# Chunk scores of the HGRN2 layer: one 32-column key stationary per chunk, in its own strip of output partitions, with the decays on the queries

## The chip, the cores and the metric

The kernel runs on one core of one Trainium2 chip. The metric is the time of one execution on the device, in microseconds (us); before the change it is 1723.18 us, the median of three runs.

## The reference, cut to what matters

A trunk of two layers over 512 tokens and a model width of 1024, in float32. Layer 0 (called layer 1 in the words of the change) is an HGRN2 gated linear recurrence with 16 heads of 128, in chunks of 32 tokens; layer 1 is a dilated attention, which the change does not touch. For one head and one chunk the recurrence is

```python
def step(state, xs):
    q_c, k_c, lf_c, v_c = xs
    b = jnp.cumsum(lf_c, axis=2)          # log of the forget gate, summed inside the chunk
    b_last = b[:, :, -1:, :]
    q_dec = q_c * jnp.exp(b)
    scores = jnp.einsum('bhcd,bhsd->bhcs', q_dec, k_c * jnp.exp(-b))
    scores = jnp.where(causal, scores, 0.0)
    o = (jnp.einsum('bhcs,bhse->bhce', scores, v_c)
         + jnp.einsum('bhcd,bhde->bhce', q_dec, state))
    state = (jnp.exp(b_last[:, :, 0, :])[..., None] * state
             + jnp.einsum('bhcd,bhce->bhde', k_c * jnp.exp(b_last - b), v_c))
    return state, o
```

The kernel works on blocks of 128 tokens, four chunks each. Inside a block it computes the scores of each chunk's queries against the keys of its own and of all earlier chunks, so the decays of the whole chunks in between have to be put on one of the two operands. The state is carried from block to block.

## The kernel before, in words

**Layout.** S = 512 tokens are ST = 4 blocks of P = 128; a block has NC = 4 chunks of CH = 32. Channels lie on the partitions, tokens run along the free axis. The 16 heads go in four rounds ("quads") of HQ = 4; `quads` (L258) loops over three rounds and writes the last one out separately (`last`).

**TensorE.** Nearly all of its work is `split_matmuls` (L418, its matmul is L422): every projection is three matmuls, with weights and activations each split into a high and a low part of type fp32r, 512 columns at a time. A head has three projection tiles, forget gate (F), query (Q) and gate (G), each computed in two halves of 12 matmuls (`head_tile`). Between the halves, `hg_body` (L610) calls `recurrence` (L599) for the head before: `scores` (L558) after the first half of F, `updates` (L572) after the second, `outputs` (L580) after the first half of Q, `norm_sum` (L593) after the second. For the last head of a round the same four stand between halves of value or output projections. `scores` has 16 matmuls of full f32: for block b and chunk j the stationary is `keys[:, b, j, 0:seen]` with seen = 32, 64, 96 or 128 key columns, the moving operand is the 32 queries of chunk j. Then three transposes (L569) turn `keys[:, b, 4, :]`, the keys decayed to the block's end, for the state update.

**VectorE and ScalarE.** Per head, ScalarE computes the forget gate, its log and its exponentials `eb` and `enb` (lines L837 to L852), VectorE the running sum (`cumulate`, L1153) and then `decays` (L1156), which makes the queries `qd`, `qs` and the four versions of the keys that `scores` reads: `keys[:, b, j, :]` holds the keys decayed up to chunk j. `A`, the decay of one whole chunk, is the last column of `eb` of that chunk. Then `mask_scores` (L1122) copies the scores out of PSUM with the causal mask, and `states` (L1132) carries the state. Each engine works through its own list in the order in which it is written, `decays` is followed by `split_lo` (L1017, the low part of a weight tile) and, further on, by `gate` and `mask_scores`. `link` makes VectorE wait for its own last result through a semaphore; there are 11 of them per head.

**What waits for what.** `scores` waits for `keys_ready` (the last of the key products, L1177), `kT_copy` on ScalarE (L802) for the transposes, `updates` for that copy, `outputs` for `q_ready`, `sT_ready` and `state_ready`. The two exponentials of a head are followed by `decays`, whose start also comes behind `hg_output` of the head before, which waits for `norm_sum` through ScalarE (L815, L817).

Of the kernel before, what the change touches and what calls it, by code (L numbers as in the profile page):

```python
# [31 lines left out]
ALU = mybir.AluOpType  # L32
# [4 lines left out]
P = 128  # L37
S = 512
# [3 lines left out]
H = W // P  # L42
HQ = 4
NQ = H // HQ
ST = S // P
# [72 lines left out]
LINKS_HG = 4 * 11  # L118
# [7 lines left out]
def program(nc, x, ln_g, hg_w_in, hg_lb, hg_norm, hg_w_out, at_w_in, at_w_out, rel_bias, final_g,  # L126
            consts, onehot, relmask, out):
    ctx = ExitStack()
    with ctx:
# [42 lines left out]
        ef, fg, kk, lnf, bb, eb, enb, qd, qs, sT = [rows[:, i, :] for i in range(10)]  # L172
        keys = sb("keys", [P, ST, NC + 1, P])
        dec = sb("dec", [P, ST, NC + 1])
# [24 lines left out]
        relmask_sb = keys[:, :, :, :].rearrange("p a b c -> p (a b c)")[0:H, 0:GROUPS * EXT]  # L199
        ext_sb = keys[:, :, :, :].rearrange("p a b c -> p (a b c)")[0:H, GROUPS * EXT:2 * GROUPS * EXT]  # L200
# [38 lines left out]
        q_ready, keys_ready, scores_done, sT_ready = sems("q_ready keys_ready scores_done sT_ready")  # L239
        kT_done, kT_ready, U_done, state_ready = sems("kT_done kT_ready U_done state_ready")  # L240
# [176 lines left out]
        def _(pe):  # L417
# [140 lines left out]
            def scores(g):  # L558

                pe.wait_ge(keys_ready, g + 1)  # L560
                for b in range(ST):
                    for j in range(NC):

                        seen = (j + 1) * CH
                        ins = nc.tensor.matmul(p_sc[0:seen, b * P + j * CH:b * P + (j + 1) * CH], keys[:, b, j, 0:seen],  # L565
                                               qd[:, b * P + j * CH:b * P + (j + 1) * CH], start=True, stop=True)
                ins.then_inc(scores_done, 1)
                for b in range(ST - 1):
                    ins = nc.tensor.transpose(p_kT[:, b * P:(b + 1) * P], keys[:, b, NC, :], ident[:, :])  # L569
                ins.then_inc(kT_done, 1)  # L570
# [9 lines left out]
            def outputs(g, h):  # L580

                pe.wait_ge(q_ready, g + 1)
                pe.wait_ge(sT_ready, g + 1)
                pe.wait_ge(state_ready, g + 1)
                for b in range(ST):
                    s = slice(b * P, (b + 1) * P)
                    ins = nc.tensor.matmul(p_O[:, s], v_sb[0][:, b, h * P:(h + 1) * P], sT[:, s],  # L587
                                           start=True, stop=(b == 0))
                    if b:
                        ins = nc.tensor.matmul(p_O[:, s], state[:, b - 1, :], qs[:, s], start=False, stop=True)  # L590
                ins.then_inc(O_done, 1)
# [424 lines left out]
        def _(dve):  # L1016
# [84 lines left out]
            step(nc.vector.memset(dec[:, :, :], 1.0))  # L1101
# [30 lines left out]
            def states(link, g):  # L1132

                dve.wait_ge(U_done, g + 1)
                link(nc.vector.tensor_copy(state[:, 0, :], p_U[:, 0:P]))
                link(nc.vector.scalar_tensor_tensor(out=state[:, 1, :], in0=state[:, 0, :], scalar=dec[:, 1, NC:NC + 1],
                                                    in1=p_U[:, P:2 * P], op0=ALU.mult, op1=ALU.add))
                nc.vector.scalar_tensor_tensor(out=state[:, 2, :], in0=state[:, 1, :], scalar=dec[:, 2, NC:NC + 1],
                                               in1=p_U[:, 2 * P:3 * P], op0=ALU.mult, op1=ALU.add)\
                    .then_inc(state_ready, 1)  # L1140
# [15 lines left out]
            def decays(link, q, h, g, low_before):  # L1156
# [5 lines left out]
                nc.vector.tensor_tensor(qd[:, :], proj[bank][:, :], eb[:, :], ALU.mult).then_inc(bank_free[bank], 1)  # L1162

                flat = keys[:, :, :, :].rearrange("p b s k -> p b (s k)")
                own = bass.AP(flat.tensor, flat.offset, [list(flat.ap[0]), [(NC + 1) * P, ST], [P + CH, NC], [1, CH]])
                after = bass.AP(flat.tensor, flat.offset + P, [list(flat.ap[0]), [(NC + 1) * P, ST], [P + CH, NC], [1, CH]])
                link(nc.vector.tensor_tensor(own, chunk(kk), chunk(enb), ALU.mult))
# [3 lines left out]
                link(nc.vector.tensor_tensor(after, own, A.broadcast_to([P, ST, NC, CH]), ALU.mult))  # L1171

                link(nc.vector.tensor_copy(dec[:, :, 1:2], A[:, :, 0, :]))

                for j in range(1, NC):
                    link(nc.vector.tensor_tensor(dec[:, :, j + 1:j + 2], dec[:, :, j:j + 1], A[:, :, j, :], ALU.mult))
                    ins = nc.vector.tensor_tensor(keys[:, :, j + 1, 0:j * CH], keys[:, :, j, 0:j * CH],  # L1177
                                                  A[:, :, j, :].broadcast_to([P, ST, j * CH]), ALU.mult)
                    if j < NC - 1:
                        link(ins)  # L1180
                    else:
                        ins.then_inc(keys_ready, 1)
                nc.vector.tensor_tensor(chunk(qs), chunk(qd), dec[:, :, 0:NC].unsqueeze(3).broadcast_to([P, ST, NC, CH]),
                                        ALU.mult).then_inc(q_ready, 1)
# [271 lines left out]
```

## Time and profile before

| | |
|---|---|
| three runs | 1716.9, 1723.18, 1723.3 us; median 1723.18 |
| span of the profiled execution, first to last instruction | 1719.9 us; its time as a run is not given apart from the three above |
| TensorE matmul busy | 1696.3 us, 99% |
| TensorE weight load busy | 1446.8 us, 84% |
| VectorE busy | 798.4 us, 46% |
| ScalarE busy | 642.7 us, 37% |
| mean granted TensorE clock | 0.982 of full speed |
| HBM traffic | 89 GB/s over the span |

The recurrence lies in the first 580 us. The busy time of TensorE is a modelled one, since matmuls overlap, so the argument below reads starts and the chain of waits, not busy shares. In the chain a matmul of full f32 is two passes of the array, two instructions; a projection matmul is one.

### The profile page before, as it was taken

The numbers are of one execution on the slowest core, as the hardware profiler recorded it, in microseconds if no ns is written. First come the engines' busy times: TensorE is split into PE (matmuls) and PEld (weight loads), VectorE is DVE, ScalarE is ACT, GpSimd is POOL, SyncE is SP. The second block draws the span as 40 slices with busy tenths as digits, with TensorE's granted clock in tenths as the row PEclk, the third lists the DMA queues.
The fourth block names the chain that finished last, engine by engine and source line by source line (L and its number), as shares of the span: only waits on it lengthen the run. The fifth ranks groups of instructions, "written<-read, shape, count | busy, mean of one in ns | idle before, by whom it ended". The sixth has DMA issues, their size and how long they took to land.

```text
span 1719.9 us, 22142 instructions
## 1 busy us (share of the span) xinstructions
PE 1696.3 (99%) x8249; PEld 1446.8 (84%) x8249; DVE 798.4 (46%) x1363; ACT 642.7 (37%) x1088; POOL 20.8 (1%) x40
## 2 busy tenths in 40 slices
PE   7999999999999999999999999999999999999997
PEld 6888888888888689888899888889888889888886
DVE  6564574556465632444433344442344442334445
ACT  4443354343344333343332333333233333233333
POOL 0000000000000000000000000000000000000000
PEclk9999999998998999999999999999999999999999
DMA  6522321321321124433314323332333333333321
GB/s 208 158 69 73 92 64 45 110 73 61 91 69 61 39 85 117 98 81 84 89 54 122 98 62 87 91 86 91 113 93 80 93 68 98 98 93 82 87 54 62
DMA packets 247998, 149.47 MB, mean 87 GB/s; under 512 B 47040, under 2 KB 227648, under 8 KB 247920
## 3 DMA queue, kind: packets, MB, share of 16 engines
q1 hardware_dynamic: 203328, 139.69, 29.4%
q0 software_dynamic: 2608, 8.39, 1.5%
q10 hardware_dynamic: 41984, 0.27, 1.3%
q8 instruction: 59, 0.97, 0.2%
q14 instruction: 19, 0.16, 0.0%
HBM read 146.02 MB, written 6.50 MB: 89 GB/s over the span
## 4 chain that ended last, share of the span: by engine, by line
PE 97%; DVE 1%; ACT 1%; issue 0%; DMA 0%; SPq 0%; DVEq 0%; ACTq 0%
PE proj L422 80%; PE inner L565 4%; PE inner L686 3%; PE inner L654 2%; PE inner L422 2%; PE inner L674 2%; PE inner L642 1%; PE inner L587 1%; PE inner L590 1%; PE inner L576 1%; PE inner L569 0%; DMA v<-x 0%; DVE v L1405 0%; PE inner L544 0%; PE inner L531 0%
## 5 line engine op out<-in xcount | busy, mean ns | idle before, releaser
L1023 DVE TENSOR_TENSOR w_lo<-raw,w_hi 128x1024 fp32r<-128x1024 f32 x252 | 308.0, 1223 | 483.2 <-ACT w_hi L735 482.1
L422 PE MATMUL proj<-u_hi,w_hi 128*128 128x512 f32 x1280 | 514.6, 402 | 0.0
L422 PE MATMUL proj<-u_hi,w_lo 128*128 128x512 f32 x1280 | 503.1, 393 | 0.0
L422 PE MATMUL proj<-u_lo,w_hi 128*128 128x512 f32 x1280 | 503.0, 393 | 0.0
L735 ACT ACTIVATE w_hi<-raw 128x1024 fp32r<-128x1024 f32 x252 | 265.3, 1053 | 133.6 <-PE proj L422 118.5
L422 PEld LDWEIGHTS proj<-u_hi,w_lo 128*128 128x128 f32 x1280 | 243.1, 190 | 52.7
L422 PEld LDWEIGHTS proj<-u_lo,w_hi 128*128 128x128 f32 x1280 | 243.7, 190 | 48.7
L422 PEld LDWEIGHTS proj<-u_hi,w_hi 128*128 128x128 f32 x1280 | 243.4, 190 | 48.8 <-issue 0.3
L422 PE MATMUL proj<-w_hi,u_hi 128*128 128x512 f32 x472 | 191.8, 406 | 6.7 <-issue 3.7
L422 PE MATMUL proj<-w_lo,u_hi 128*128 128x512 f32 x472 | 189.2, 401 | 0.0
L422 PE MATMUL proj<-w_hi,u_lo 128*128 128x512 f32 x472 | 188.9, 400 | 0.0
L422 PEld LDWEIGHTS proj<-w_hi,u_hi 128*128 128x128 f32 x472 | 121.8, 258 | 18.9 <-issue 8.9
L422 PEld LDWEIGHTS proj<-w_hi,u_lo 128*128 128x128 f32 x472 | 121.8, 258 | 9.4
L422 PEld LDWEIGHTS proj<-w_lo,u_hi 128*128 128x128 f32 x472 | 122.1, 259 | 8.5
L969 ACT ACTIVATE qk<-proj 128x512 f32<-128x512 f32 x96 | 57.0, 594 | 161.7 <-PE proj L422 161.7
L899 ACT ACTIVATE rows<-rows,negm 128x256 f32<-128x256 f32 (+1 forms) x128 | 61.9, 484 | 140.8 <-DVE negm L1303 135.6
L422 PE MATMUL proj<-y_hi,w_hi 128*128 128x512 f32 x256 | 103.4, 404 | 0.9 <-DVE sg L1112 0.7
L422 PE MATMUL proj<-y_lo,w_hi 128*128 128x512 f32 x256 | 100.2, 391 | 0.0
L422 PE MATMUL proj<-y_hi,w_lo 128*128 128x512 f32 x256 | 100.1, 391 | 0.0
L741 ACT ACTIVATE v<-proj 128x512 f32<-128x512 f32 x59 | 35.1, 596 | 138.8 <-PE proj L422 127.2
L1205 DVE TENSOR_TENSOR hT<-hT,proj 128x512 f32<-128x512 f32 x80 | 54.4, 686 | 69.0 <-PE proj L422 68.7
L565 PEld LDWEIGHTS inner<-rows,keys 128*32 128x32 f32 (+3 forms) x512 | 53.6, 156 | 13.1 <-issue 5.3
(156 smaller groups left out, 1497.0 us busy)
## 6 DMA issues: line engine op xcount, KB each, us to landing
raw<-at_w_in SPq DMA_DIRECT2D x160, 512.0 KB, 4.1
raw<-hg_w_in SPq DMA_DIRECT2D x64, 512.0 KB, 4.2
raw<-hg_w_out SPq DMA_DIRECT2D x16, 512.0 KB, 3.6
raw<-at_w_out SPq DMA_DIRECT2D x16, 512.0 KB, 4.4
v<-x SPq DMA_DIRECT2D x4, 512.0 KB, 6.5
bias_tiles<-ext_rows POOLq DMA_DIRECT2D x1, 2048.0 KB, 11.8
bias_tiles<-ext_rows POOLq DMA_DIRECT2D x2, 1024.0 KB, 17.6
bias_n<-bias_tiles POOLq DMA_DIRECT2D x16, 128.0 KB, 4.1
```

Source lines behind the costliest of these rows:

```text
L422: ins = nc.tensor.matmul(bank[:, :], stationary(a), moving(b), start=(first and n == 0), stop=(last and n == 2))
L565: ins = nc.tensor.matmul(p_sc[0:seen, b * P + j * CH:b * P + (j + 1) * CH], keys[:, b, j, 0:seen], qd[:, b * P + j * CH:b * P + (j + 1) * ...
L576: ins = nc.tensor.matmul(p_U[:, b * P:(b + 1) * P], kT[:, b, :], v_sb[0][:, b, h * P:(h + 1) * P], start=True, stop=True)
L654: ins = nc.tensor.matmul(p_S[r // 2][:, ((r % 2) * 2 + i) * P:((r % 2) * 2 + i + 1) * P], qk[:, 2 + 2 * i, s], qk[:, 3 + 2 * i, s], start= ...
L674: ins = nc.tensor.transpose(p_T[n % 2][:, (i % 4) * P:(i % 4 + 1) * P], src, ident[:, :])
L686: ins = nc.tensor.matmul(o, vals, pT[:, i, :], start=(i == 0), stop=(i == len(TILES) - 1), skip_group_check=True)
L735: nc.scalar.activation(w["hi"][:, slot, :], raw[:, slot, :], ACT.Copy).then_inc(hi_ready, 1)
L741: nc.scalar.activation(v_sb[group][:, (e - (0 if q is None else layer.heads)) % ST, :], value_bank(layer, q, e)[:, :], ACT.Copy).then_inc( ...
L899: nc.scalar.activation(probs[:, i, 0:n], probs[:, i, 0:n], ACT.Exp, bias=negm[:, i:i + 1], accum_out=stat[:, i // ST, 1, b:b + 1]).then_in ...
L969: nc.scalar.activation(o, src, ACT.Copy, scale=QSCALE if i in (Q0, Q1, Q2) else 1.0)\
L1023: nc.vector.tensor_tensor(w["lo"][:, slot, :], raw[:, slot, :], w["hi"][:, slot, :].bitcast(F32), ALU.subtract).then_inc(w_ready, 1)
L1205: nc.vector.tensor_tensor(hT[:, k, :], hT[:, k, :], proj[bank][:, :], ALU.add)\
```

## The change

Each chunk's keys are made once, decayed to the end of their own chunk (`aft`), and stand in TensorE once per block: 32 columns, whose results go to the 32 output partitions of that chunk. They meet the queries of their own chunk and of all later ones in one matmul, 128, 96, 64 or 32 columns. The decays between chunks are on the queries: `qx[:, b, r, j, :]` is chunk j's queries with the decays of the r − 1 chunks before it (r = 0: with the own chunk's decay divided out again, by `undo`), and the moving operand takes r = 0 for the own chunk, 1, 2, 3 for later ones: n pieces of 32 with a step of 160 elements (`q_steps`). The keys at the block's end, `kend`, are made apart and have a semaphore of their own (`kend_ready`), for which TensorE waits between the scores and the transposes. `outputs` reads `q_steps(b, 1, 0, NC)` in place of `qs`. Nothing else in the order of the work changes.

```diff
 Q0, K0, Q1, K1, Q2, K2, GA = range(7)
-LINKS_HG = 4 * 11
+LINKS_HG = 4 * 5
 LINKS_AT = 4 * 7
...
         rows = sb("rows", [P, 10, S])
-        ef, fg, kk, lnf, bb, eb, enb, qd, qs, sT = [rows[:, i, :] for i in range(10)]
-        keys = sb("keys", [P, ST, NC + 1, P])
-        dec = sb("dec", [P, ST, NC + 1])
+        ef, fg, kk, lnf, bb, eb, enb, kend, spare_row, sT = [rows[:, i, :] for i in range(10)]
+
+        qx = sb("qx", [P, ST, NC + 1, NC, CH])
+        aft = sb("aft", [P, S])
+        tail = sb("tail", [P, ST, NC + 1])
+        undo = sb("undo", [P, ST, NC])
...
+        def q_steps(b, r, j, n):
+
+            at = ((b * (NC + 1) + r) * NC + j) * CH
+            return bass.AP(qx_flat.tensor, qx_flat.offset + at, [list(qx_flat.ap[0]), [(NC + 1) * CH, n], [1, CH]])
...
+        kend_ready = sem("kend_ready")
...
                 pe.wait_ge(keys_ready, g + 1)
                 for b in range(ST):
-                    for j in range(NC):
-
-                        seen = (j + 1) * CH
-                        ins = nc.tensor.matmul(p_sc[0:seen, b * P + j * CH:b * P + (j + 1) * CH], keys[:, b, j, 0:seen],
-                                               qd[:, b * P + j * CH:b * P + (j + 1) * CH], start=True, stop=True)
+                    for c in range(NC):
+
+                        own = slice(c * CH, (c + 1) * CH)
+                        to = p_sc[own, b * P + c * CH:(b + 1) * P].rearrange("p (j c) -> p j c", c=CH)
+                        ins = nc.tensor.matmul(to, aft[:, b * P + c * CH:b * P + (c + 1) * CH],
+                                               q_steps(b, 0, c, NC - c), start=True, stop=True)
                 ins.then_inc(scores_done, 1)
+                pe.wait_ge(kend_ready, g + 1)
                 for b in range(ST - 1):
-                    ins = nc.tensor.transpose(p_kT[:, b * P:(b + 1) * P], keys[:, b, NC, :], ident[:, :])
+                    ins = nc.tensor.transpose(p_kT[:, b * P:(b + 1) * P], kend[:, b * P:(b + 1) * P], ident[:, :])
                 ins.then_inc(kT_done, 1)
...
                     if b:
-                        ins = nc.tensor.matmul(p_O[:, s], state[:, b - 1, :], qs[:, s], start=False, stop=True)
+                        ins = nc.tensor.matmul(p_O[:, s].rearrange("p (j c) -> p j c", c=CH), state[:, b - 1, :],
+                                               q_steps(b, 1, 0, NC), start=False, stop=True)
                 ins.then_inc(O_done, 1)
...
+            step(nc.vector.memset(tail[:, :, :], 1.0))
...
                 link(nc.vector.tensor_copy(state[:, 0, :], p_U[:, 0:P]))
-                link(nc.vector.scalar_tensor_tensor(out=state[:, 1, :], in0=state[:, 0, :], scalar=dec[:, 1, NC:NC + 1],
+                link(nc.vector.scalar_tensor_tensor(out=state[:, 1, :], in0=state[:, 0, :], scalar=tail[:, 1, 0:1],
                                                     in1=p_U[:, P:2 * P], op0=ALU.mult, op1=ALU.add))
-                nc.vector.scalar_tensor_tensor(out=state[:, 2, :], in0=state[:, 1, :], scalar=dec[:, 2, NC:NC + 1],
+                nc.vector.scalar_tensor_tensor(out=state[:, 2, :], in0=state[:, 1, :], scalar=tail[:, 2, 0:1],
                                                in1=p_U[:, 2 * P:3 * P], op0=ALU.mult, op1=ALU.add)\
                     .then_inc(state_ready, 1)
...
                 A = chunk(eb)[:, :, :, CH - 1:CH]
                 dve.wait_ge(proj_done, number + 1)
                 dve.wait_ge(eb_ready, 2 * g + 2)
-                nc.vector.tensor_tensor(qd[:, :], proj[bank][:, :], eb[:, :], ALU.mult).then_inc(bank_free[bank], 1)
-
-                flat = keys[:, :, :, :].rearrange("p b s k -> p b (s k)")
-                own = bass.AP(flat.tensor, flat.offset, [list(flat.ap[0]), [(NC + 1) * P, ST], [P + CH, NC], [1, CH]])
-                after = bass.AP(flat.tensor, flat.offset + P, [list(flat.ap[0]), [(NC + 1) * P, ST], [P + CH, NC], [1, CH]])
-                link(nc.vector.tensor_tensor(own, chunk(kk), chunk(enb), ALU.mult))
+                grown = undo[:, :, :].unsqueeze(3).broadcast_to([P, ST, NC, CH])
+                qstep = lambda r: qx[:, :, r, r - 1:NC, :]
+                nc.vector.tensor_tensor(qstep(1), chunk(proj[bank]), chunk(eb), ALU.mult).then_inc(bank_free[bank], 1)
+                nc.vector.reciprocal(undo[:, :, :], A[:, :, :, 0])
+                nc.vector.tensor_copy(tail[:, :, 3:4], A[:, :, 3, :])
+                link(nc.vector.tensor_tensor(aft[:, :], kk[:, :], enb[:, :], ALU.mult))
                 if low_before:
                     y_low(g - 1, h - 1)
 
-                link(nc.vector.tensor_tensor(after, own, A.broadcast_to([P, ST, NC, CH]), ALU.mult))
-
-                link(nc.vector.tensor_copy(dec[:, :, 1:2], A[:, :, 0, :]))
-
-                for j in range(1, NC):
-                    link(nc.vector.tensor_tensor(dec[:, :, j + 1:j + 2], dec[:, :, j:j + 1], A[:, :, j, :], ALU.mult))
-                    ins = nc.vector.tensor_tensor(keys[:, :, j + 1, 0:j * CH], keys[:, :, j, 0:j * CH],
-                                                  A[:, :, j, :].broadcast_to([P, ST, j * CH]), ALU.mult)
-                    if j < NC - 1:
-                        link(ins)
-                    else:
-                        ins.then_inc(keys_ready, 1)
-                nc.vector.tensor_tensor(chunk(qs), chunk(qd), dec[:, :, 0:NC].unsqueeze(3).broadcast_to([P, ST, NC, CH]),
-                                        ALU.mult).then_inc(q_ready, 1)
+                nc.vector.tensor_tensor(qx[:, :, 0, :, :], qstep(1), grown, ALU.mult)
+                nc.vector.tensor_tensor(tail[:, :, 2:3], tail[:, :, 3:4], A[:, :, 2, :], ALU.mult)
+                nc.vector.tensor_tensor(chunk(aft), chunk(aft), A.broadcast_to([P, ST, NC, CH]), ALU.mult)
+                link(nc.vector.tensor_tensor(qstep(2), qx[:, :, 1, 1:NC, :],
+                                             A[:, :, 0:NC - 1, :].broadcast_to([P, ST, NC - 1, CH]), ALU.mult))
+                nc.vector.tensor_tensor(tail[:, :, 1:2], tail[:, :, 2:3], A[:, :, 1, :], ALU.mult)
+                nc.vector.tensor_tensor(qstep(3), qx[:, :, 2, 2:NC, :],
+                                        A[:, :, 0:NC - 2, :].broadcast_to([P, ST, NC - 2, CH]), ALU.mult)\
+                    .then_inc(keys_ready, 1)
+                dve.wait_ge(keys_ready, g + 1)
+                nc.vector.tensor_tensor(tail[:, :, 0:1], tail[:, :, 1:2], A[:, :, 0, :], ALU.mult)
+                nc.vector.tensor_tensor(chunk(kend), chunk(aft),
+                                        tail[:, :, 1:NC + 1].unsqueeze(3).broadcast_to([P, ST, NC, CH]), ALU.mult)\
+                    .then_inc(kend_ready, 1)
+                nc.vector.tensor_tensor(qstep(4), qx[:, :, 3, 3:NC, :],
+                                        A[:, :, 0:NC - 3, :].broadcast_to([P, ST, NC - 3, CH]), ALU.mult)\
+                    .then_inc(q_ready, 1)
```

On TensorE the place is one head's scores, behind the last projection matmul of the half before; the columns are line, operation, names, and stationary columns x moving columns. Before, blocks of four matmuls, four times:

```order
L422 MATMUL proj<-u_hi,w_lo 128x512
L560 ISA
L565 MATMUL inner<-rows,keys 32x32
L565 MATMUL inner<-rows,keys 64x32
L565 MATMUL inner<-rows,keys 96x32
L565 MATMUL inner<-rows,keys 128x32
```

With the change (`rows` in L581 is `kend`):

```order
L432 MATMUL proj<-u_hi,w_lo 128x512
L570 ISA
L576 MATMUL inner<-qx,aft 32x128
L576 MATMUL inner<-qx,aft 32x96
L576 MATMUL inner<-qx,aft 32x64
L576 MATMUL inner<-qx,aft 32x32
L581 MATMUL inner<-ident,rows 128x128 x3
```

The count is the same, 16 matmuls; the stationary is always 32 wide, and the moving operand is long where it was always 32.

On VectorE the place is `decays` of one head, from the product of query and `eb` to the last product. Before (`rows` is `qd`, `eb`, `kk`, `enb` or `qs`; a REGISTER_ALU row belongs to a wait of `link`):

```order
L1162 TENSOR_TENSOR rows<-proj,rows 128x512
L1167 TENSOR_TENSOR keys<-rows 128x16x32
L1171 TENSOR_TENSOR keys<-keys,rows 128x16x32
L1173 COPY dec<-rows 128x4
L1176 TENSOR_TENSOR dec<-dec,rows 128x4
L1177 TENSOR_TENSOR keys<-keys,rows 128x4x32
L1177 TENSOR_TENSOR keys<-keys,rows 128x4x64
L1177 TENSOR_TENSOR keys<-keys,rows 128x4x96
L1183 TENSOR_TENSOR rows<-rows,dec 128x512
```

With the change:

```order
L1177 TENSOR_TENSOR qx<-proj,rows 128x4x128
L1178 RECIPROCAL undo<-rows 128x16
L1179 COPY tail<-rows 128x4
L1180 TENSOR_TENSOR aft<-rows 128x512
L1184 TENSOR_TENSOR qx<-qx,undo 128x4x128
L1185 TENSOR_TENSOR tail<-tail,rows 128x4
L1186 TENSOR_TENSOR aft<-aft,rows 128x512
L1187 TENSOR_TENSOR qx<-qx,rows 128x4x96
L1190 TENSOR_TENSOR qx<-qx,rows 128x4x64
L1195 TENSOR_TENSOR rows<-aft,tail 128x512
L1198 TENSOR_TENSOR qx<-qx,rows 128x4x32
```

`keys_ready` was signalled by the last L1177 of before; now it is signalled by L1190, `kend_ready` by L1195 and `q_ready` by L1198. (Each L1176 of before stands three times, between the L1177s; the small products L1189 and L1194 of the change are not shown.)

## Rows read from the trace of the kernel before

**Rows 1.** The page: busy times, TensorE's clock by slice, the chain.

```profile
PE 1696.3 (99%) x8249; PEld 1446.8 (84%) x8249; DVE 798.4 (46%) x1363; ACT 642.7 (37%) x1088; POOL 20.8 (1%) x40
...
PEclk9999999998998999999999999999999999999999
...
PE 97%; DVE 1%; ACT 1%; issue 0%; DMA 0%; SPq 0%; DVEq 0%; ACTq 0%
```

**Rows 2.** The chain of waits, a head undisturbed: start us, length us, what.

```profile
113.40 3.67 PE inner L565 x32
117.08 0.36 PE inner L569 x3
117.44 2.77 PE proj L422 x12
...
128.43 8.20 PE proj L422 x36
136.63 4.22 PE inner L565 x32
```

**Rows 3.** The chain, other heads' scores.

```profile
63.86 3.67 PE inner L565 x32
...
88.64 4.12 PE inner L565 x32
...
392.50 4.17 PE inner L565 x32
...
418.84 3.67 PE inner L565 x32
```

**Rows 4.** Stretches: us, busy (count) of PE, PEld, DVE, ACT, POOL, granted clock, DMA, GB/s.

```profile
67.70:71.10 3.40, 3.40 (x10) 2.73 (x9) 0.74 (x4) 0.49 (x1) 0.00 (x0) 0.50 0.16 48
117.50:120.90 3.40, 3.40 (x19) 2.91 (x18) 0.51 (x4) 1.06 (x2) 0.00 (x0) 1.00 0.50 155
139.40:146.20 6.80, 6.80 (x23) 5.61 (x24) 1.56 (x5) 0.74 (x2) 0.00 (x0) 0.50 0.40 130
...
733.99:737.30 3.31, 3.31 (x33) 3.31 (x32) 0.45 (x1) 0.00 (x0) 0.00 (x0) 1.00 0.41 116
```

**Rows 5.** The chain, two stretches of full-f32 matmuls of the attention.

```profile
733.99 3.35 PE inner L686 x30
737.34 1.52 PE inner L642 x8
```

**Rows 6.** TensorE in order of time, first block's scores: start us, us.

```profile
63.79 0.25 PE L565 MATMUL inner<-rows,keys 128*32 128x32 f32 x2
...
63.97 0.59 PE L565 MATMUL inner<-rows,keys 128*64 128x32 f32 x4
...
64.20 0.58 PE L565 MATMUL inner<-rows,keys 128*96 128x32 f32 x4
```

**Rows 7.** VectorE in order of time, `decays` of one head: start us, us.

```profile
131.36 0.69 DVE L1162 TENSOR_TENSOR rows<-proj,rows 128x512 f32<-128x512 f32 x1
131.96 0.68 DVE L1167 TENSOR_TENSOR keys<-rows 128x512 f32<-128x512 f32 x1
132.68 0.69 DVE L1171 TENSOR_TENSOR keys<-keys,rows 128x512 f32<-128x512 f32 x1
133.41 0.17 DVE L1173 COPY dec<-rows 128x4 f32<-128x4 f32 x1
...
133.81 0.29 DVE L1177 TENSOR_TENSOR keys<-keys,rows 128x128 f32<-128x128 f32 x1
...
134.34 0.42 DVE L1177 TENSOR_TENSOR keys<-keys,rows 128x256 f32<-128x256 f32 x1
...
135.00 0.56 DVE L1177 TENSOR_TENSOR keys<-keys,rows 128x384 f32<-128x384 f32 x1
```

**Rows 8.** ScalarE in order of time, around the same head's scores.

```profile
115.80 0.63 ACT L828 ACTIVATE eg<-eg 128x512 f32<-128x512 f32 x1
117.48 0.49 ACT L804 ACTIVATE kT<-inner 128x384 f32<-128x384 f32 x1 [1.04 <-PE inner L569]
```

More of the change, by code:

```diff
@@ L198, in program @@
         onehot_sb = pT[:, :, :].rearrange("p a b -> p (a b)")[0:BUCKETS, 0:GROUPS * EXT]
-        relmask_sb = keys[:, :, :, :].rearrange("p a b c -> p (a b c)")[0:H, 0:GROUPS * EXT]
-        ext_sb = keys[:, :, :, :].rearrange("p a b c -> p (a b c)")[0:H, GROUPS * EXT:2 * GROUPS * EXT]
+        qx_flat = qx[:, :, :, :, :].rearrange("p a r j c -> p (a r j c)")
+        relmask_sb = qx_flat[0:H, 0:GROUPS * EXT]
+        ext_sb = qx_flat[0:H, GROUPS * EXT:2 * GROUPS * EXT]
+        def q_steps(b, r, j, n):
+            at = ((b * (NC + 1) + r) * NC + j) * CH
+            return bass.AP(qx_flat.tensor, qx_flat.offset + at, [list(qx_flat.ap[0]), [(NC + 1) * CH, n], [1, CH]])
         relb_sb = bias_n[0:BUCKETS, 0:GROUPS * H]
@@ L1100, in _ @@
             step(nc.vector.memset(sT[:, :], 0.0))
-            step(nc.vector.memset(dec[:, :, :], 1.0))
+            step(nc.vector.memset(tail[:, :, :], 1.0))
             dve.wait_ge(const_loaded[4], 32)
```

## The prediction

> **What bounds the kernel now.** I read the page first: TensorE has matmuls in flight for 99% of the span and the chain that ended last lies on it for 97% [rows 1]. That means that VectorE, ScalarE and DMA matter only where TensorE would come to wait for them, and that what the change takes from TensorE's own path comes off the time. TensorE's clock row shows two slices below full among the early ones [rows 1]. Next the chain in order of time [rows 2]: one head of the recurrence is a period of 23.23 us from one scores stage to the next (136.63 − 113.40), with 3.67 us for the 32 passes of the scores, 0.36 for the three transposes, the rest in projections and small stages, no gap. There are 16 such stages. Then the same view for other heads [rows 3]: from 63.86 to 88.64 the period is 24.78, from 392.50 to 418.84 it is 26.34, with the same work. The stretches [rows 4] say why: right after the scores at 63.86 the granted clock is 0.50 of full, 1.2 GHz in place of 2.4, for 3.4 us, and only 10 projection passes fall in it; after the undisturbed stage it is 1.00, and after the stage at 136.63 it is 0.50 for 6.8 us. Asking the same of all 16 stages gives 5 with no fall, 8 with a fall of some 3.4 us and 3 of some 6.8 us. So the scores cost twice: their own time, and a clock that falls behind 11 of them.
>
> **The passes on TensorE.** A full-f32 matmul is two passes. What limits a pass: 30 passes with 128 loaded and 128 moving columns take 3.35 us [rows 5], 0.112 each. Eight passes with 2 x 128 + 6 x 256 = 1792 moving columns take 1.52 us [rows 5], 0.848 ns per moving column, though the loads stay at 128: so a load goes beside the stream before it, and the longer of the two counts. Before, a block loads 2 x (32 + 64 + 96 + 128) = 640 columns to stream 32 each; at 0.112 per 128 loaded that is 0.56 us, but a block takes 3.67 / 4 = 0.918 [rows 2]. The other 0.36 lies in three changes of the stationary's width class (128 to 32, 32 to 64, 64 to 96), 0.12 us each. Two of them can be read off the starts [rows 6]: the pair of 32-column passes should take 0.056 us and the next starts 0.18 later, the 64-column pair should take 0.11 and the next starts 0.23 later.
>
> With the change a block streams 2 x (128 + 96 + 64 + 32) = 640 columns, and loads only 32 a pass, 0.028 us. If the passes follow one another, a block takes 640 x 0.848 ns = 0.543 us. If only a strip's own two passes follow one another, and the next strip's first pass starts as soon as its 32 columns are loaded, it takes 320 x 0.848 ns + 4 x 0.028 = 0.383. No row shows two strips at work, so I take the middle, 0.463, and keep both as ends. The width changes now twice a head, at the start and back at the transposes: 0.24. Stage: 4 x 0.463 + 0.24 = 2.09 us in place of 3.67, **1.58 saved, x 16 = 25.3 us** (ends: 2.41 us and 20.2; 1.77 us and 30.4).
>
> **The clock.** Two stretches to compare. Behind the old scores it falls; there TensorE streamed 1024 columns in 3.67 us, 279 per us. In the attention's 30 passes it stays at 1.00 [rows 4, 5] with 3840 columns in 3.35 us, 1146 per us. The new stage streams 2560 columns in 2.09 us, 1225 per us, and is shorter. It is near the second, so I take it that the clock stays up behind all 16. What that gives: a short fall costs 24.78 − 23.23 = 1.55 us, a long one 26.34 − 23.23 = 3.11 [rows 2, 3]; 8 x 1.55 + 3 x 3.11 = **21.7 us**. Ends: nothing, and all of it.
>
> **VectorE.** `decays` up to `keys_ready` takes 135.56 − 131.36 = 4.20 us now [rows 7]. From the starts in the same rows an operation that nothing links costs its length less 0.09 (131.36 to 131.96), a linked one its length plus 0.04 (131.96 to 132.68). The new list: product with eb 0.60, reciprocal of 16 columns 0.1, copy 0.08, linked product 0.72, two 512-column products 1.20 with a small one 0.08, linked step 2 (384 columns) 0.60, small one 0.08, step 3 (256 columns) 0.42: 3.9 us, so the scores may start some 0.3 earlier. They stood ready 1.1 us before their use anyway [rows 2, 7], which hides this. `kend_ready` follows 0.04 + 0.08 + 0.69 = 0.8 us later, half a microsecond after the old `keys_ready` and still 0.6 before the scores start; the transposes read it only behind the scores. So the added wait costs nothing; should the cover go, TensorE would stand at most those 0.8 us a head. `q_ready` comes another 0.29 − 0.09 = 0.2 behind that, at 4.9 us, where it came at 4.20 + 0.6 = 4.8, and is used only by the outputs, two half tiles behind the scores. Queued behind on VectorE are a weight tile, `bound_gate`, `gate` and `mask_scores`; 0.1 later, against waits of this engine that last microseconds. Zero, then. In the last head, where `decays` is on the chain, the 0.3 is kept within the rounding.
>
> **What gets tight.** ScalarE does its gate exponentials until 116.43 and only then copies the transposes; now it waits 1.04 us for them [rows 8]. The transposes will end about 115.9, the copy from 116.43 to 116.92, and the updates begin at 113.40 + 2.09 + 0.36 + 2.77 = 118.6: 1.7 us of room. The chain from `norm_sum` to `keys_ready` lies behind the shortened stage and keeps its distance: 7.1 of the 8.2 us of the next 36 projection matmuls [rows 2, 7]. I find no term here.
>
> **Strided queries.** The scores and the three state products now read pieces of 32 columns with gaps between. No row has such a moving operand. The nearest, contiguous ones, give zero; one end is a few per cent of 2.09 us, 1 or 2 us in all, the other a gain I exclude, since nothing reads less. Zero.
>
> **Sum.** 25.3 + 21.7 = 47.0 us. The profiled span becomes 1719.9 − 47.0 = 1672.9. The median of the runs lies 3.3 above the span, and I keep that: 1676 us, 2.7% less. The three runs before lie 6.4 us apart, as much as four short falls of the clock; a kernel without falls should scatter less. Half a per cent, 8.6 us, is about what a measurement of this kernel can tell from no change.
>
> **The rivals.**
> - *The strips work wholly side by side.* Then strip 0's two passes of 128 set a block: 2 x 128 x 0.848 ns = 0.217, the stage is 1.11 us, 2.56 x 16 = 41.0 saved, and with the clock 62.7: **1660.5 us**. For it: different strips share no output partition. Against it: the passes are in one queue and each strip's second must wait for its first. The Trainium skill, "TensorE: Matmul & The Clock Gate", Part 3, says that matmuls whose outputs lie in different 32-partition strips run concurrently, a few ns apart, and that starts and ends stay in program order; by it the stage lies between my low end and this. No row here shows it.
> - *The clock falls as before.* The array is filled over 32 of its 128 columns only, where in the attention it is full; if that is what counts, the new stage is as idle as the old. Only the passes are saved: **1698 us**. Against it: the stage is shorter by two fifths, and what surrounds it is dense.
> - *Each change of strip empties the array* (the other side). Then all 16 matmuls of a stage pay what a change of width pays now, 0.12, and the 0.028 of a load that is no longer hidden: 2.17 + 16 x 0.148 + 0.12 = 4.66 us in place of 3.67, and the clock falls as it does: 1723.2 + 15.8 = **1739 us**. It decides from (3.67 − 2.17 − 0.12) / 16 = 0.086 us per change of strip; just about there nothing changes, 1723. For it: the gap at each of the three width changes. Against it: a strip keeps the width. The Trainium skill, "TensorEngine Tiling (Array Packing)", Key Properties, says that a change of tiling mode drains TensorE, and a change of tile alone does not; the first half agrees with the 0.12, the second no row shows.
>
> **How the numbers follow.** My forecast, with the scores stage between 1.77 and 2.41 us and the clock up (1671 to 1682), 0.68. Wholly side by side 0.10. Clock still falling 0.10. Strip changes that cost: 0.12, of which 0.05 for slower, 0.07 for about no change. Faster by over 0.5%: 0.88; within: 0.07; slower: 0.05. The range goes from the side-by-side case to just beyond the falling clock, 1661 to 1700 us; the strip-change cases are left out.
>
> **What the profile after would show.** The 32 passes of the scores at some 2.1 us in the chain (1.8 if strips overlap in part, 2.4 if not, over 3.5 if changes drain); periods of 21.6 us for every inner head, and none at 23 or above; granted clock 1.00 behind each stage; no idle time of TensorE for `kend`; VectorE's `decays` to its last product 4.9 us. A stage over 3 us, or periods that still come in three lengths, would make the prediction wrong.

## The result, and the profile after

The changed kernel takes **1660.53 us** (median of four runs, 1659.6 to 1661.12); the kernel before 1723.24 us (median of four, 1716.9 to 1728.69). The ratio is 0.9644, with a 95% interval from 0.9614 to 0.9674: faster by 62.7 us, 3.6%. The forecast was 1676 us, in a range from 1661 to 1700, so the time lies half a microsecond below the range's lower end. It is the number of the first rival, 1660.5 us. The spread of the runs, 12 us before, is 1.5 us after.

The page of the changed kernel, the parts that answer to [rows 1]:

```profile
PE 1634.7 (99%) x8249; PEld 1392.4 (84%) x8249; DVE 800.4 (48%) x1395; ACT 641.3 (39%) x1088; POOL 20.8 (1%) x40
...
PEclk9999999999999999999999999999999999999999
...
PE 96%; DVE 2%; ACT 1%; issue 0%; DMA 0%; SPq 0%; DVEq 0%; ACTq 0%
```

TensorE still has the path and the same number of instructions; in the row of the clock no slice is below 9 any more. The chain of waits of the changed kernel over one inner head (start us, length us, what), against [rows 2]:

```profile
105.04 0.99 PE inner L576 x18
106.03 0.48 PE inner L581 x3
106.50 2.78 PE proj L432 x12
109.29 0.67 PE inner L588 x6
...
117.50 8.20 PE proj L432 x36
125.70 0.99 PE inner L576 x18
...
127.17 3.05 PE proj L432 x12
```

(x18 counts the passes that lie on the chain; the others of the 32 run beside them.) The scores take 0.99 us where they took 3.67, and the transposes 0.48 where they took 0.36, since the way back from 32-wide to 128-wide stationaries now lies before them. The period is 125.70 − 105.04 = 20.66 us, against 23.23 in a head of before whose clock stayed up: 2.57 x 16 = 41.1 us. The rest, 62.7 − 41.1 = 21.6 us, is about what the clock's falls cost by [rows 2, 3], 21.7. It does not come out to a tenth: the runs before scatter by 12 us, and the spans of the two profiled executions differ by 61.0 us (1719.9 and 1658.9).

The last row is a small new loss. Behind the last head of each of the first three rounds the next 12 projection matmuls take 3.05 us, where they take 2.78 behind the other heads, 0.8 us in all. TensorE's loads wait there for VectorE's low part of a weight tile, as the list of waits shows; in the kernel before this wait does not occur between 40 and 580 us.

```profile
PEld proj L432 <- DVE w_lo L1036: 1.3, 3, 0.4
```

Granted clock in stretches of the changed kernel (the columns as in [rows 4]):

```profile
106.50:110.00 3.50, 3.50 (x20) 2.96 (x19) 2.86 (x8) 2.33 (x4) 0.00 (x0) 1.00 0.65 178
...
40.00:510.00 470.00, 469.48 (x2667) 387.73 (x2666) 304.00 (x574) 223.15 (x325) 1.11 (x2) 1.00 0.31 92
```

In the whole stretch with the 16 scores stages the clock is 1.00, 2.4 GHz; only behind it, at 541.9 us, the trace has one more short fall. VectorE in order of time, `decays` of one head of the changed kernel, against [rows 7]:

```profile
99.77 0.69 DVE L1177 TENSOR_TENSOR qx<-proj,rows 128x512 f32<-128x512 f32 x1
...
103.22 0.42 DVE L1190 TENSOR_TENSOR qx<-qx,rows 128x256 f32<-128x256 f32 x1
103.67 0.17 DVE L1194 TENSOR_TENSOR tail<-tail,rows 128x4 f32<-128x4 f32 x1
103.75 0.69 DVE L1195 TENSOR_TENSOR rows<-aft,tail 128x512 f32<-128x512 f32 x1
104.35 0.28 DVE L1198 TENSOR_TENSOR qx<-qx,rows 128x128 f32<-128x128 f32 x1
```

`keys_ready` comes 3.87 us after the start (3.9 forecast, 4.20 before), `kend_ready` at 104.44 and `q_ready` at 104.63, 4.86 us (4.9 forecast). The scores of this head start at 104.97, as the first row of TensorE in order of time shows:

```profile
104.97 1.06 PE L576 MATMUL inner<-qx,aft 128*32 128x128 f32 x32
105.96 0.44 PE L581 MATMUL inner<-ident,rows 128*128 128x128 f32 x2
```

All 32 passes lie within 1.06 us (the two rows overlap, since the recorded length of a pass, up to 0.298 us, is longer than the time to the next start). The recorded starts of the single passes say more. Strip 0's eight passes, of 128 columns each, start about 0.109 us apart, and the last of them 0.79 us after the first; seven steps of 0.109 are 0.76. All other passes start before it. Strip 3's last pass, issued after it, starts at 0.53, so 0.26 us earlier.

### The profile page after: what moved, and what is told of

It is laid out like the page before. It is cut to its first block, busy times and chain, and to the rows that moved or that the text cites. A ratio compares the mean times of both kernels' runs of the same rounds, so it can differ in the third digit from the quotient of the medians.

```text
span 1658.9 us, 22066 instructions
## 1 busy us (share of the span) xinstructions
PE 1634.7 (99%) x8249; PEld 1392.4 (84%) x8249; DVE 800.4 (48%) x1395; ACT 641.3 (39%) x1088; POOL 20.8 (1%) x40
## 4 chain that ended last, share of the span: by engine, by line
PE 96%; DVE 2%; ACT 1%; issue 0%; DMA 0%; SPq 0%; DVEq 0%; ACTq 0%
PE proj L432 82%; PE inner L699 3%; PE inner L667 2%; PE inner L432 2%; PE inner L687 2%; PE inner L655 1%; PE inner L576 1%; PE inner L599 1%; PE inner L602 1%; PE inner L588 1%; PE inner L581 0%; DMA v<-x 0%; DVE v L1421 0%; PE inner L554 0%; PE inner L541 0%
## 5 line engine op out<-in xcount | busy, mean ns | idle before, releaser
L432 PEld LDWEIGHTS proj<-y_hi,w_hi 128*128 128x128 f32 x256 | 48.1, 188 | 12.3 <-issue 3.0
```

What stands on the lines that cost most here:

```text
L432: ins = nc.tensor.matmul(bank[:, :], stationary(a), moving(b), start=(first and n == 0), stop=(last and n == 2))
```

## The experiments

In all of them the theory is that each of the four strips works through its own passes, and that the stage is as long as its fullest strip (theory 1). The ratios are to the kernel before, run beside each.

### One strip for all

```diff
-                        own = slice(c * CH, (c + 1) * CH)
+                        own = slice(0, CH)
```

> The changed kernel with the results of all 16 score matmuls sent to output partitions 0 to 31; the other strips' scores are left out of the result. Same passes, same columns, one strip. Theory 1 (the four strips work as four separate queues, and strip 0's eight passes of 128 columns set the stage): with one strip all 32 passes follow one another, 640 columns x 0.848 ns x 4 blocks = 2.17 us in place of 0.87, so 1.3 us more a head, 21 us in all, 1681 us, if the clock stays up. Theory 2 (the gain comes from the fewer changes of width and the longer moving operands, the place of the output does not matter): 1660.5 us. If a dense stage of 2.2 us in a quarter of the array lets the clock fall, some 1.55 us more per head: up to 1706 us.

Measured: 1679.66 us (1679.29 to 1680.2), ratio 0.9747 [0.9723, 0.9771]. The chain of waits of this kernel:

```profile
108.06 2.35 PE inner L576 x32
```

With the same passes, the same stationaries and the same moving operands in one strip, the stage takes 2.35 us, 1.36 more than in four. That is near the forecast's upper end (2.41, of which the way back to 128-wide stationaries, 0.12, stands in the next row of the chain), and 2560 columns x 0.848 ns are 2.17. So the place of the output is what lets the passes overlap. The clock stays up here too, so 1680 is what the kernel would have taken by the end "one after another".

### One strip, everything twice

```diff
-                        own = slice(c * CH, (c + 1) * CH)
+                        own = slice(0, CH)
...
-                        ins = nc.tensor.matmul(to, aft[:, b * P + c * CH:b * P + (c + 1) * CH],
+                        for _ in range(2):
+                            ins = nc.tensor.matmul(to, aft[:, b * P + c * CH:b * P + (c + 1) * CH],
```

> As one_strip, and each of the 16 matmuls is issued twice: a stage of 64 passes one after another, 4.34 us, longer than the stage of the kernel before (3.67), dense in columns, in a quarter of the array. Theory 1a (the clock falls behind stretches that stream few columns, however much of the array is filled): no fall, 16 x (4.34 - 0.87) = 55.5 us over the changed kernel, 1716 us. Theory 1b (what is filled of the array counts): the clock falls behind most stages, 1.55 to 3.1 us each, 1738 us or more.

Measured: 1715.6 us (1714.34 to 1717.27), ratio 0.9953 [0.9938, 0.9968]. The chain, and the stretch with all 16 stages:

```profile
110.64 4.58 PE inner L577 x64
115.22 0.48 PE inner L582 x3
```

```profile
40.00:590.00 550.00, 549.46 (x3275) 464.86 (x3274) 319.36 (x597) 232.75 (x338) 1.12 (x2) 1.00 0.27 80
```

The stage is now longer than that of before, 4.58 against 3.67 us, and fills a quarter of the array, and still the granted clock is 1.00 throughout. In the kernel before, TensorE streamed 279 columns per us in the stages and the clock fell behind 11 of 16; here it is 5120 / 4.58 = 1118. So neither the length of the stage nor the share of the array that it fills made the clock fall, and theory 1b, the second rival's condition, is out. The old stage differs in two more things at once, few columns and twelve changes of the stationary's width, each with a pause of 0.12 us; no run here changes one of them without the other, so which of them counts stays open.

### The kernel before, its scores in two pieces

```diff
+                    if mid and k == half * KT // 2 + 2:
+                        mid()
                     ins = split_matmuls(proj[bank], lambda a: w[a][:, slot, k * P:(k + 1) * P],
...
-                        head_tile(HG, q, HG.per_head * h + half // 2, half % 2)
+                        rest = (lambda: scores(head(q, h - 1), (2, 3))) if h and half == 1 else None
+                        head_tile(HG, q, HG.per_head * h + half // 2, half % 2, rest)
```

`scores` takes the blocks as an argument: (0, 1) at its old place and (2, 3) in the middle of the next half; the value and output projections got the same.

> The kernel before with the same 16 score matmuls per head in two pieces of 8, six (or fewer) projection matmuls between them, nothing else moved. Theory 1 (the clock falls behind a scores stage because TensorE streams few columns for 3.67 us on end): no stretch is that long any more, no falls, 21.7 us less than before, 1701.5 us, with the scores themselves as long as they were. Theory 2 (the falls have another cause, or the 21.7 us were misread and the scores' passes carry the whole gain): 1723 us, and the clock still at half behind the stages.

Measured: 1700.79 us (1700.72 to 1701.04), ratio 0.9880 [0.9838, 0.9922]. The chain, and the stretch with all stages:

```profile
109.91 1.84 PE inner L572 x16
111.75 1.48 PE proj L422 x6
113.22 1.84 PE inner L572 x16
115.06 0.36 PE inner L578 x3
...
133.22 1.84 PE inner L572 x16
```

```profile
40.00:570.00 530.00, 529.76 (x2751) 437.07 (x2750) 312.97 (x560) 229.82 (x333) 1.12 (x2) 1.00 0.28 82
```

The scores take 2 x 1.84 = 3.68 us, as they did, the period is 133.22 − 109.91 = 23.31, as in a head of before without a fall (23.23), and the clock stays at 1.00. This is the clock's share of the gain by itself: 22.4 us off the 1723.2 us of the first comparison, 19.6 off the kernel before beside it, whose runs scattered from 1714 to 1728. The forecast's term was 21.7. It also shows why the runs before scattered and these four, within 0.3 us, do not: the falls differ from run to run. Of the runs before beside it the fastest, 1713.98 us, has a mean granted clock of 0.987 and the slowest, 1728.19 us, one of 0.977; these four all have 0.996.

### Strips 2 and 3 twice, strip 0 twice

```diff
-                        ins = nc.tensor.matmul(to, aft[:, b * P + c * CH:b * P + (c + 1) * CH],
+                        for _ in range(2 if c >= 2 else 1):
+                            ins = nc.tensor.matmul(to, aft[:, b * P + c * CH:b * P + (c + 1) * CH],
```

(and `c == 0` in place of `c >= 2` for the second kernel)

> The changed kernel with the matmuls of strips 2 and 3 (64 and 32 queries) issued twice: 2 x 96 x 4 = 768 columns more a head, 0.65 us if passes of different strips shared time. Theory 1 (each strip its own queue, strip 0 sets the stage with 0.87 us, strip 2 then needs 0.87, strip 3 0.43): no change, 1660.5 us. Theory 2 (passes follow one another or overlap only with their neighbours in the order of issue): 5 to 10 us more, 1666 to 1671 us.

> The changed kernel with strip 0's matmuls (128 queries) issued twice: 1024 columns more a head. Theory 1: strip 0 sets the stage, 0.87 us more a head, 13.9 us in all, 1674.4 us. If something else sets it (another strip, the issue of instructions), less than half of that, below 1667 us.

Measured: 1662.1 us (1661.19 to 1662.4), ratio 0.9643 [0.9619, 0.9666], with strips 2 and 3 twice; 1674.65 us (1673.32 to 1675.34), ratio 0.9717 [0.9693, 0.9741], with strip 0 twice. In the chains, first the one and then the other:

```profile
104.32 1.02 PE inner L577 x26
```

```profile
106.38 1.86 PE inner L577 x25
```

768 columns more in strips 2 and 3 make the stage 0.03 us longer; 1024 more in strip 0 make it 0.87 us longer, which is its own columns (1024 x 0.848 ns = 0.87). Only the fullest strip counts, as theory 1 has it. In time the first kernel is 1.6 us above the 1660.5 that were expected; the rival asked for 5 to 10.

### The order of issue

```diff
-                for b in range(ST):
-                    for c in range(NC):
+                for c in range(NC):
+                    for b in range(ST):
```

> The changed kernel with the two loops of the scores exchanged: all of strip 0's matmuls are issued first, then strip 1's, 2's, 3's. Theory 1 with a long look-ahead (a pass starts as soon as its own strip is free, whatever was issued before): 0.87 us as it is, 1660.5 us. Theory 1 with starts in order of issue: strip 1's first pass starts only when strip 0's last has started, at 0.76 us, and needs 0.65 from there: 1.41 or more, 0.54 us more a head, 1669 us.

Measured: 1666.14 us (1665.68 to 1667.42), ratio 0.9681 [0.9639, 0.9722]. TensorE in order of time, one stage:

```profile
104.66 1.52 PE L576 MATMUL inner<-qx,aft 128*32 128x128 f32 x32
106.11 0.55 PE L581 MATMUL inner<-ident,rows 128*128 128x128 f32 x3
```

1.52 us, 0.46 more than in the order by block; 0.54 were expected if passes start in the order of issue, none if the look-ahead reached over all of them. So TensorE does start passes ahead of others issued before them, but not from far behind. In the recorded starts strip 1's first pass comes at 0.47 us, when five of strip 0's eight have started (in the order of issue it would be 0.79); strip 2's first comes at 0.83, and strip 3's last, which ends the stage's starts, at 1.32. The mixed order of the changed kernel is worth 5.6 us.

### The queries' gaps, and the second wait

The first kernel reads contiguous queries in the scores and in the state products; the decays between chunks are thereby left out or put on the wrong chunks. The second signals once, when `kend` is ready.

```diff
-                                               q_steps(b, 0, c, NC - c), start=True, stop=True)
+                                               qx[:, b, 1, 0:NC - c, :], start=True, stop=True)
```

```diff
-                pe.wait_ge(kend_ready, g + 1)
...
-                    .then_inc(kend_ready, 1)
+                    .then_inc(keys_ready, 1)
```

> The changed kernel with contiguous moving operands (pieces of 32 with no gap) of the same number of columns, for the scores and the state products; the decays between chunks are thereby left out or put on the wrong chunks. Theory: gaps of 160 elements between pieces of 32 cost nothing, 1660.5 us. Rival: the gapped reading costs a few per cent of the passes; then 1 to 2 us less, 1659 us.

> The changed kernel with keys_ready signalled only when kend is ready too, and no second wait on TensorE. Theory (VectorE has both ready half a microsecond before the scores start, except in the last head, where they are on the chain): 1660.5 us, at most 1 us more. Rival (the separate wait is what keeps TensorE from standing): up to 0.8 us a head, 1673 us.

Measured: 1660.75 us (1659.5 to 1661.79), ratio 0.9649 [0.9607, 0.9690], and 1660.68 us (1659.5 to 1660.92), ratio 0.9644 [0.9603, 0.9686]. Both are the changed kernel's time. Pieces of 32 elements with a step of 160 from one to the next cost nothing that can be measured (the stage is 0.99 us in the chain of both), and the separate wait for `kend` saves nothing: VectorE is ready before. Only once, in the last head, does TensorE wait for the products in this kernel, 1.0 us in the list of waits (0.4 in the changed kernel).

### The mask at once

```diff
                     decays(link, q, h, g, early)
+                    mask_scores(g)
...
                         gate(HG, q, h - 1, before, 3 * (h - 1) + G_)
-                        mask_scores(before)
```

> The changed kernel with mask_scores moved to directly behind decays, so that VectorE stands waiting when the scores end and its start shows when their signal arrives. The signal is carried by the last pass issued, of strip 3, which in the changed kernel starts 0.26 us before strip 0's last pass. Theory A (a signal is held until all passes issued before have ended): the mask starts about 1.1 us behind the stage's first pass. Theory B (it comes with its own pass): the mask starts some 0.3 us earlier, before strip 0 has ended. The time: within 1 us of 1660.5 if VectorE has the room that it seems to have; what it does after the mask comes up to 2.4 us later.

Measured: 1689.49 us (1687.49 to 1690.35), ratio 0.9800 [0.9778, 0.9823]. TensorE and VectorE in order of time:

```profile
106.87 1.06 PE L576 MATMUL inner<-qx,aft 128*32 128x128 f32 x32
...
108.02 0.87 DVE L1141 TENSOR_TENSOR rows<-inner,causal 32x128 f32<-32x128 f32 x4 [1.47 <-PE inner L576]
```

The mask starts 1.15 us after the first pass, 0.09 after the recorded end of the last (106.87 + 1.06). The pass that carries the signal, strip 3's last, has its own recorded end at 0.73 us, 0.42 before the mask starts; for comparison, the copy of the transposes in [rows 2, 8] starts 0.04 us after the recorded end of the last transpose. So the signal came only when the passes issued before had ended, as theory A has it. (The recorded ends are modelled, so the 0.33 us between the two theories is read from modelled times.) The expected time failed, by 29 us: VectorE had no room for this. Its next operations came 2.3 us later (1.47 of waiting, 0.87 of mask). Behind them came `bound_gate`, ScalarE's gate and the copy of the transposes, for which TensorE now waits. The list of waits of this kernel:

```profile
PEld inner L588 <- ACT kT L817: 24.4, 13, 2.1
...
PE inner L588 <- ACT kT L817: 18.9, 13, 1.7
```

### Level strips: what it is worth, and a whole version

The first kernel puts chunk c of every other block in strip 3 − c, so that all strips stream 640 columns; those blocks' results are wrong. The second does it whole.

```diff
-                        own = slice(c * CH, (c + 1) * CH)
+                        strip = NC - 1 - c if b % 2 else c
+                        own = slice(strip * CH, (strip + 1) * CH)
```

```diff
-                for b in range(ST - 1):
+                for c in range(NC):
+                    to = slice((NC - 1 - c) * CH, (NC - c) * CH)
+                    nc.tensor.matmul(p_kT[to, P:2 * P], kend[:, P + c * CH:P + (c + 1) * CH], ident[:, :],
+                                     start=True, stop=True)
+                for b in range(0, ST - 1, 2):
                     ins = nc.tensor.transpose(p_kT[:, b * P:(b + 1) * P], kend[:, b * P:(b + 1) * P], ident[:, :])
...
+                for to, at in swapped(layer is HG and b % 2):
+                    ins = nc.scalar.activation(v_sb[group][to, b, :], value_bank(layer, q, e)[at, :], ACT.Copy)
```

> The changed kernel with the strips of every other block in reverse (chunk c in strip 3 - c), so that each strip streams the same number of columns, 320 x 2 in four blocks; keys and values of these blocks no longer stand on the same partitions, so those blocks' outputs are left wrong, it only shows what levelling would be worth. Theory 1 (a stage is as long as its fullest strip): 640 x 0.848 ns = 0.54 us in place of 0.87, 0.33 x 16 = 5.2 us less, 1655.3 us. Rival (issue or look-ahead bounds it once the strips are level): 1658 to 1660.5 us.

> A whole version of strips_level: in every other block of the HGRN2 layer chunk c's scores go to strip 3 - c, the values of these blocks are copied out of PSUM with their four 32-partition pieces in reverse (ScalarE, four instructions in place of one), the block's keys for the state update are turned by four 32-column f32 matmuls with the identity in four strips instead of one transpose, and the mask is one VectorE operation with both masks in place of four. Strips level: 0.33 us less a head, the four identity matmuls 0.1 more than the transpose: 0.2 x 16 = 3.5 us less than the changed kernel, 1657 us, if ScalarE's 1.8 us more per copied value block stay hidden. Rival: the copy of the transposes on ScalarE, which had 0.8 us of room, or the value copies come onto the path: 1660.5 us or more.

> The changed kernel once more, on the same chip as levelled, for the comparison: 1660.5 us within 1 us.

Measured: 1655.92 us (1654.69 to 1657.63), ratio 0.9607 [0.9586, 0.9628], for the first; 1660.21 us (1658.25 to 1660.59), ratio 0.9641 [0.9623, 0.9658], for the whole version, beside 1660.87 us (1660.06 to 1661.26), ratio 0.9643 [0.9626, 0.9661], for the changed kernel. The stage in the chain of the first kernel:

```profile
104.92 0.68 PE inner L577 x17
```

The chain of the whole version:

```profile
103.88 0.68 PE inner L577 x17
104.56 0.24 PE inner L583 x8
104.80 0.37 PE inner L586 x2
...
123.98 1.14 DVE w_lo L1049
125.11 0.60 DVE y_lo L1226
...
126.05 1.15 DVE w_lo L1049
```

Level strips take 0.68 us against 0.99, as forecast, and the first kernel gets 4.6 us of the expected 5.2. In the whole version 0.13 of the 0.31 us goes into the eight passes with the identity (0.24 + 0.37 against 0.48). By the starts of the scores an inner head's period is 20.35 us in the first kernel and 20.49 in the whole version, against 20.67.

From the last head of a round to the first of the next, level strips gain nothing: 64.45 to 64.48 us in either kernel, 64.46 in the changed one. There the chain now goes from the norm's sum through ScalarE and VectorE, by way of `decays` and the low parts of the weights, back to TensorE. The wait for the low parts is the one that the changed kernel already has, 1.3 us in all; in the whole version it is 1.9. What is new in the whole version is one wait for ScalarE's copy of the values:

```profile
PEld proj L432 <- DVE w_lo L1049: 1.9, 3, 0.6
PEld proj L432 <- ACT v L767: 1.5, 1, 1.5
```

The difference between the whole version and the changed kernel, 0.7 us, is not measurable; no version with right results here beats it clearly.

## Why the prediction was right or wrong

- **The passes on TensorE: that the passes cost less is right, how far the strips overlap is wrong, and this carries the whole miss.** The step that failed is "If only a strip's own two passes follow one another, and the next strip's first pass starts as soon as its 32 columns are loaded", 0.383 us per block, taken for the lower end, with the middle, 0.463, taken as the value because no row showed two strips at work. The hidden assumption was one queue in which a strip's waiting second pass holds back the next strip. The stage takes 0.99 us, the level of 0.217 per block of the first rival, and the doubled strips show that only the fullest strip counts. Saved are (3.67 − 0.99) x 16 = 42.9 us, less the 0.12 x 16 = 1.9 that the transposes give back: 41.0 us in place of 25.3. The difference, 15.7 us, is that between the forecast of 1676 us and the measured time.
- **The clock: right.** 21.7 us forecast; 21.6 is what is left of the result after the periods, and the kernel before with its scores in two pieces gains 20 to 22 us by this alone. The stretch of the attention was the right one to compare with: at 1118 columns per us the clock stayed up even in a quarter of the array. Whether the few columns or the pauses at the changes of width count is not shown.
- **The changes of width: right.** 0.12 us for the way back is the 0.48 against 0.36 of the transposes, and 0.12 for the way there is what the stage takes beyond strip 0's columns (0.99 against 0.87). A change of strip costs nothing, so the rival on the slower side falls.
- **The added wait, the gaps: zero, as forecast,** each by an experiment. `keys_ready` and `q_ready` come when they were said to.
- **What gets tight: nearly right.** TensorE does not stand for the copy of the transposes in the inner heads (its list of waits has it once, 1.0 us). But "I find no term here" missed a small one: the wait for VectorE's low part of a weight tile, once in each of three rounds, 0.8 us in all. And the room is small, as `mask_at_once` found, where I again took VectorE's waits for room that could be spent.
- **The rivals.** The first came true, with a chance of 0.10 where the forecast had 0.68. Its "Against it", that the passes are in one queue, was an assumption with no row behind it. The Trainium skill, "TensorE: Matmul & The Clock Gate", Part 3, says that matmuls in different strips run concurrently, and the traces agree: 0.99 us for what takes 2.35 us in one strip. It also says that matmuls start and end in program order. The recorded starts do not agree: strip 3's last pass starts 0.26 us before strip 0's last, which was issued before it.
- **The sum.** 42.9 − 1.9 + 21.7 = 62.7 us is the measured difference. That it fits to a tenth is luck: the runs before scatter by 12 us, the profiled spans differ by 61.0, and the 0.8 us of the new wait are not in it.

## What to carry to other kernels

Here a matmul with 32 output columns cost its own strip only: four of them, with outputs in four different 32-partition strips, ran side by side, and the stage was as long as its fullest strip, 0.99 us where one strip took 2.35. They have to be issued mixed; strip by strip it was 0.46 us more. When a stage of small matmuls stands between dense ones, look at the granted clock behind it: breaking the one of 3.67 us here in two, with no operation saved, was worth 1.2%. And a wait of an engine is room only as far as the next engine's wait behind it allows.

## What the runs showed of the hardware that I had not expected

- Passes of different strips start out of the order of issue: 32 passes with 2560 columns in 1.06 us from the first start to the last recorded end, against 2.42 us in one strip. The reach is limited: issued strip by strip they take 1.52 us.
- The signal on the last pass issued, which belongs to the emptiest strip, arrives only when the fullest has ended: the waiting mask started 0.09 us after the last recorded end, 0.42 us after that of the pass with the signal.
- A dense stage of 4.58 us in a quarter of the array leaves the clock at 1.00, where it fell to 0.50 behind 11 of 16 stages with 1024 columns in 3.67 us.
- Four f32 matmuls of 32 columns with the identity, side by side, take 0.24 us for what one transpose does in about 0.12.
